# Key and query lengths through logarithms in the decay exponents, and a new order of units around the delta rule

## What is computed

```
qkv = silu(causal_depthwise_conv(proj[..., :1536], conv_qkv));  q, k, v = split(qkv)
q = q * rsqrt(sum(q^2) + 1e-6) * 128 ** -0.5        # per token and head
k = k * rsqrt(sum(k^2) + 1e-6)
g = -(exp(a_log) * softplus(a + dt_bias));  beta = sigmoid(bt);  g_cum = cumsum(g) in the chunk
decay = exp(where(causal, g_cum[i] - g_cum[j], -inf))
kk = strict_lower((beta k) k^T * decay)
u, k_cum = (I + kk)^-1 [v * beta, beta k * exp(g_cum)]
qk = (q k^T) * decay;  q_dec = q * exp(g_cum);  k_end = k * exp(g_cum[last] - g_cum)
for each chunk: v_new = u - k_cum S;  o = q_dec S + qk v_new
                S = S * exp(g_cum[last]) + k_end^T v_new
o = o * rsqrt(mean(o^2) + 1e-6) * gdn_norm;   y_a = o * silu(z)
```

## Time and profile before

| | |
|---|---|
| Median of 3 runs | 1255.66 us (1255.56 to 1256.26) |
| Profiled execution | 1255.7 us, span 1254.0 us |
| TensorE matmul busy | 1213.0 us (97% of the span) |
| VectorE, ScalarE, GpSimd busy | 390.5, 243.5, 148.7 us |
| DMA | 453.45 MB, mean 362 GB/s |
| Token mixer | to about 318 us |
| Experts | from about 340 us to 1246 us |

### The profile page before, as it was taken

One profiled execution on the slowest core, in us unless ns is written; L12 is line 12 of the kernel. 1 busy time (PEld: TensorE's weight loads), 2 busy tenths in 40 slices (PEclk: granted clock), 3 DMA queues, 4 the chain that ended last, 5 costly groups with the idle time before them and its releaser, 6 DMA issues.

```text
span 1254.0 us, 17233 instructions
## 1 busy us (share of the span) xinstructions
PE 1213.0 (97%) x7155; PEld 613.1 (49%) x7155; DVE 390.5 (31%) x768; ACT 243.5 (19%) x402; POOL 148.7 (12%) x106
## 2 busy tenths in 40 slices
PE   8999999999999999999999999999999999999995
PEld 8999999998733333333333333333333333333332
DVE  6675633335522222222222222222222222222224
ACT  5764354544210000000000000000010000000001
POOL 7454323555100000000000000000000000000000
PEclk9999999999999999999999999999999999999999
DMA  9644231875899999999999999999999999999994
GB/s 335 221 148 143 70 136 67 330 292 201 353 409 429 428 429 428 427 429 429 429 428 429 429 429 428 429 428 430 428 429 427 427 427 428 429 427 428 428 427 198
DMA packets 53388, 453.45 MB, mean 362 GB/s; under 512 B 6925, under 2 KB 7002, under 8 KB 28762
## 3 DMA queue, kind: packets, MB, share of 16 engines
q1 hardware_dynamic: 53338, 452.71, 87.0%
HBM read 451.64 MB, written 1.05 MB: 361 GB/s over the span
## 4 chain that ended last, share of the span: by engine, by line
PE 78%; DMA 8%; SPq 5%; DVE 3%; ACT 3%; issue 2%; POOL 0%; DVEq 0%; ACTq 0%
PE bank L1419 29%; PE bank L1491 15%; DMA late<-in_w_gate_up_dram 8%; PE bank L1209 6%; SPq L807 5%; PE bank L1210 5%; PE bank L1211 5%; PE bank L1504 4%; PE bank L1390 4%; PE bank L1405 2%; PE bank L1479 1%; ACT late L1181 1%; ACT w_hi L1069 1%; PE bank L1499 1%; DMA raw<-in_w_mem_kv_dram 0%
## 5 line engine op out<-in xcount | busy, mean ns | idle before, releaser
L1419 PE MATMUL bank<-late 128*64 128x512 f32 x1536 | 343.5, 595 | 5.4 <-DMA late<-in_w_gate_up_dram 5.4
L1491 PE MATMUL bank<-late 128*64 128x512 f32 x1024 | 229.6, 601 | 6.0 <-ACT late L1181 6.0
L1419 PEld LDWEIGHTS bank<-late 128*64 128x64 f32 x1536 | 106.7, 137 | 223.2 <-issue 209.6
L1491 PEld LDWEIGHTS bank<-late 128*64 128x64 f32 x1024 | 71.3, 138 | 142.4 <-issue 128.6
L1209 PE MATMUL bank<-act_hi,w_hi 128*128 128x256 f32 x448 | 129.5, 289 | 1.9 <-DVE early L1699 1.4
L1210 PE MATMUL bank<-act_lo,w_hi 128*128 128x256 f32 x448 | 125.8, 281 | 0.0
L1211 PE MATMUL bank<-act_hi,w_lo 128*128 128x256 f32 x448 | 125.7, 281 | 0.0
L1834 DVE TENSOR_SCALAR late<-bank 128x512 f32<-128x512 f32 x32 | 22.1, 692 | 308.9 <-PE bank L1419 308.9
L1419 PE MATMUL bank<-raw,late 128*64 128x512 f32 x512 | 116.7, 598 | 1.5 <-DMA raw<-in_w_gate_up_dram 1.5
L770 POOL TENSOR_TENSOR w_lo<-raw,w_hi 128x1024 fp32r<-128x1024 f32 x33 | 81.9, 2483 | 102.1 <-ACT w_hi L1069 102.0
L1209 PEld LDWEIGHTS bank<-act_hi,w_hi 128*128 128x128 f32 x448 | 84.3, 188 | 4.1 <-DVE early L1699 2.0
(11 more groups left out here) (321 smaller groups left out, 1186.4 us busy)
## 6 DMA issues: line engine op xcount, KB each, us to landing
late<-in_w_gate_up_dram SPq DMA_DIRECT2D x96, 2048.0 KB, 37.1
late<-in_w_down_dram SPq DMA_DIRECT2D x64, 2048.0 KB, 36.5
raw<-in_w_gate_up_dram SPq DMA_DIRECT2D x32, 2048.0 KB, 35.2
raw<-in_w_in_dram SPq DMA_DIRECT2D x8, 2048.0 KB, 9.0
early<-in_w_in_dram SPq DMA_DIRECT2D x6, 2048.0 KB, 8.1
raw<-in_w_br_dram SPq DMA_DIRECT2D x3, 2048.0 KB, 7.6
raw<-in_w_mem_kv_dram SPq DMA_DIRECT2D x8, 512.0 KB, 11.2
raw<-in_w_o_dram SPq DMA_DIRECT2D x1, 2048.0 KB, 8.5
```

Source lines behind the costliest of these rows:

```text
L1419: ins = mm(bk[64 * c:64 * c + 64, :], x_slotT[:, k % 4, 64 * (k // 4):64 * (k // 4) + 64], w[:, kk, at + 512 * c:at + 512 * (c + 1)], star ...
L1491: ins = mm(ps[3][64 * c:64 * c + 64, :], hidT[:, kk, 64 * q:64 * q + 64], w[:, kk, c * 512:(c + 1) * 512], start=(q == 0 and kk == 0), sto ...
```

## The change

The lengths of k and q are no longer multiplied into k and q. The sum of squares of k goes through a logarithm: half of it is added to g_cum (`log_k`), which enters the exponents of decay and of k_end; exp(-0.5 log) times beta (`beta_k`) takes beta's place where beta stood for k. The sum of squares of q acts only on the epsilon of the last norm (`o_eps`), since that norm takes any factor of a row out. The step lengths is gone, with its 16 matmuls and its VectorE and ScalarE work, and norms now writes one column for each (token tile, head) and not 128.

The squares are made by GpSimd, one head at a time, during qkv 1 to 8 (12 operations for 8 heads). The first half of the step order is new: norms stands right after qkv 11, then xc 0, logs, xc 1, the exponential and log decay, xc 2, scalars, xc 3, decay, gc 0, ScalarE's part of decay, gc 1, gc 2, **scores, gc 3, tokens, gb 0, lx0**, gb 1, lx1, gb 2, xlx1, gb 3, lx2, qm 0, xlx2, qm 1, lx3, qm 2, xlx3, qm 3, lx4, z 0, xlx4, z 1, lx5, z 2, xlx5, z 3, kcum. The z slots of weights move behind qm accordingly. Only ScalarE's parts of norms and decay stand one unit behind their products (steps `ga`).

```diff
-    ["scalars", "decay", "norms", "lengths", "scores", "tokens"]
+    ["norms", "scalars", "decay", "scores", "tokens"]
...
-    order += [("qkv", 0), ("qkv", 1), ("ab", 0), ("qkv", 2), ("abT", 0), ("qkv", 3), ("decay functions",)]
-    order += [("qkv", 4), ("qkv", 5), ("log decay",), ("qkv", 6), ("qkv", 7)] + [("g", "scalars"), ("qkv", 8), ("qkv", 9), ("g", "decay")]
-    order += [("qkv", 10), ("qkv", 11)]
...
-    long = [(kind, n) for kind in ("z", "xc", "gc", "gb", "qm") for n in range(4)]
+    order += [("qkv", 0), ("qkv", 1), ("ab", 0), ("qkv", 2), ("abT", 0)] + [("qkv", n) for n in range(3, 12)]
+    order += [("decay functions",), ("g", "norms")]
+    long = [(kind, n) for kind in ("xc", "gc", "gb", "qm", "z") for n in range(4)]
+    at = {("xc", 0): [("logs",)], ("xc", 1): [("ga", "norms"), ("log decay",)], ("xc", 2): [("g", "scalars")],
+          ("xc", 3): [("g", "decay")], ("gc", 0): [("ga", "decay")], ("gc", 1): []}
     for unit in long:
-        order += [unit]
-        if unit not in (("xc", 0), ("xc", 2)):
-            order += [("g", g.pop(0))]
+        order += [unit] + (at[unit] if unit in at else [("g", g.pop(0))])
         if unit[0] == "qm":
             order += [("score", unit[1])] + ([("soft", unit[1] - 1)] if unit[1] else [])
...
# ScalarE
+                act.wait_ge(g_act, GA["norms"] - 1)
+                a.activation(beta_k, log_k, ACT.Exp, scale=-0.5).then_inc(g_act, 1)
+            elif name == "logs":
+                a.activation(t_b, t_b, ACT.Ln, bias=1.0).then_inc(ab_act, 1)
                 act.wait_ge(g_pe, GP["norms"])
-                for t in range(NT):
-                    for n in range(2):
-                        ins = a.activation(inv_norm[:, t, 4 * n:4 * n + 4], ps[4 + 2 * t + n][:, 0::P], ACT.Sqrt,
+                a.activation(log_k, ps[5][:, 0:NPB].rearrange("p (t h) -> p t h", t=NT), ACT.Ln,
...
# TensorE
-                        ins = mm(out4(t * 2 * H + n), squares[:, n, t * P:(t + 1) * P], ones[:], start=True, stop=True)
-            elif name == "lengths":
-                pe.wait_ge(g_dve, GD["norms"])
-                for n in range(2 * H):
-                    for t in range(NT):
-                        ins = mm(ps[4 + n // 2][:, (n % 2) * T + t * P:(n % 2) * T + (t + 1) * P],
-                                 spread(inv_norm, t, n), ident[:], start=True, stop=True)
+                        ins = mm(ps[4 + n // H][:, at:at + 1], squares[:, n, t * P:(t + 1) * P], ones[:, 0:1], start=True, stop=True)
...
             elif name == "scores":
-                pe.wait_ge(g_dve, GD["lengths"])
+                pe.wait_ge(g_dve, GD["decay"])
+                pe.wait_ge(g_act, GA["decay"] - 2)
...
# VectorE, step scalars
+                v.wait_ge(g_act, GA["norms"])
+                step(d.tensor_tensor(beta_k, beta_k, beta, ALU.mult))
                 v.wait_ge(g_pe, GP[name])
                 step(d.tensor_copy(gcum, ps[3][:, 0:NPB].rearrange("p (t h) -> p t h", t=NT)))
+                step(d.scalar_tensor_tensor(out=log_k, in0=log_k, scalar=0.5, in1=gcum, op0=ALU.mult, op1=ALU.add))
...
# VectorE, step scores (the eight operations behind the wait are unchanged)
                 v.wait_ge(g_act, GA["decay"])
-                step(d.tensor_tensor(bexp, bexp, beta, ALU.mult))
+                step(d.tensor_tensor(bexp, bexp, beta_k, ALU.mult))
                 step(d.tensor_copy(chunk_decay, expg[:, :, CHUNK - 1::CHUNK]))
-                v.wait_ge(g_act, GA[name])
-                d.reciprocal(inv_norm, inv_norm).then_inc(g_dve, 1)
...
# VectorE, step olen
-                d.tensor_reduce(o_ss, LT, AX.X, ALU.add).then_inc(g_dve, 1)
+                step(d.tensor_reduce(o_ss, LT, AX.X, ALU.add))
+                d.scalar_tensor_tensor(out=o_ss, in0=o_ss, scalar=1.0 / DH, in1=o_eps.rearrange("p t h -> p (t h)"),
+                                       op0=ALU.mult, op1=ALU.add).then_inc(g_dve, 1)
...
# GpSimd
+                if s[0] == "qkv" and 1 <= s[1] <= 2 * H:
+                    c = s[1] - 1
+                    pool.wait_ge(silu_done, c + 1)
+                    if c < H:
+                        for k in range(2):
+                            src = halves(qkvT[:, c, :])[:, :, 1 - k, :]
+                            ins = eng.tensor_tensor(halves(squares[:, c, :])[:, :, k, :], src, src, ALU.mult)
+                    else:
+                        ins = eng.tensor_tensor(squares[:, c, :], qkvT[:, c, :], qkvT[:, c, :], ALU.mult)
+                    ins.then_inc(squared, 1)
...
# VectorE
-                    if c == 11:
-                        v.wait_ge(silu_done, 12)
-                        d.tensor_tensor(squares, qkvT[:, 0:2 * H, :], qkvT[:, 0:2 * H, :], ALU.mult).then_inc(g_dve_sq, 1)
```

More of the change, by code:

```diff
@@ L110, in mixer_schedule @@
     order += [("ab split",)]
[L111 to L116 removed]
+    order += [("qkv", 0), ("qkv", 1), ("ab", 0), ("qkv", 2), ("abT", 0)] + [("qkv", n) for n in range(3, 12)]
+    order += [("decay functions",), ("g", "norms")]
+    g = [s for s in GDN_STEPS if s not in ("norms", "scalars", "decay", "olen", "onorm")]
+    long = [(kind, n) for kind in ("xc", "gc", "gb", "qm", "z") for n in range(4)]
+    at = {("xc", 0): [("logs",)], ("xc", 1): [("ga", "norms"), ("log decay",)], ("xc", 2): [("g", "scalars")],
+          ("xc", 3): [("g", "decay")], ("gc", 0): [("ga", "decay")], ("gc", 1): []}
     for unit in long:
[L118 to L120 removed]
+        order += [unit] + (at[unit] if unit in at else [("g", g.pop(0))])
         if unit[0] == "qm":
             order += [("score", unit[1])] + ([("soft", unit[1] - 1)] if unit[1] else [])
[L123 removed]
+        if unit == ("z", 0):
+            order += [("soft", H - 1)]
     attention = [("pT", 0), ("pT", 1), ("ym", 0), ("pT", 2), ("ym", 1), ("pT", 3), ("ym", 2), ("ym", 3)]
@@ L127, in mixer_schedule @@
         order += [attention.pop(0)]
-        order += [("g", s) for s in g[:2 if len(g) > KD - n else 1]]
-        g = g[2 if len(g) > KD - n else 1:]
+        if len(g) >= KD - n:
+            order += [("g", g.pop(0))]
     assert not g and not attention
@@ L448, in hybrid_layer @@
             GP[name] = gp
-            ga += {"lx0": 0, "decay": 3, "norms": 1, "tokens": 1, "kcum": 1, "olen": 1}.get(name, 1 if name.startswith(("lx", "state")) else 0)
+            ga += {"lx0": 0, "decay": 3, "norms": 2, "tokens": 1, "kcum": 1, "olen": 1}.get(name, 1 if name.startswith(("lx", "state")) else 0)
             GA[name] = ga
-            gd += {"lx0": 1, "scalars": 1, "decay": 1, "norms": 1, "lengths": 1, "scores": 1, "tokens": 1, "olen": 2, "kcum": 1, "vnew0": 0, "state3": 0}.get(
+            gd += {"lx0": 1, "scalars": 1, "decay": 1, "norms": 1, "scores": 1, "tokens": 1, "olen": 2, "kcum": 1, "vnew0": 0, "state3": 0}.get(
                 name, 1 if name.startswith(("xlx", "vnew", "state")) else 0)
@@ L520, in chunk_T @@
                 return a[:, p % H, (p // H) * P:(p // H + 1) * P]
-            if name == "scalars":
+            if name == "norms":
+                pe.wait_ge(squared, 2 * H)
+                pe.wait_ge(h_split, 2 * NT)
+                for n in range(2 * H):
+                    for t in range(NT):
+                        at = t * H + n % H
+                        ins = mm(ps[4 + n // H][:, at:at + 1], squares[:, n, t * P:(t + 1) * P], ones[:, 0:1], start=True, stop=True)
+            elif name == "scalars":
                 pe.wait_ge(g_dve_scal, 1)
@@ L530, in pe_gdn @@
                 pe.wait_ge(g_dve, GD["scalars"])
-                pe.wait_ge(h_split, 2 * NT)
                 for p in range(NPB):
@@ L534, in pe_gdn @@
                 for p in range(NPB):
[L535 to L537 removed]
+                    ins = mm(out4(NPB + p), spread(beta_k, p // H, p % H), ident[:], start=True, stop=True)
+            elif name == "scores":
                 pe.wait_ge(g_dve, GD["decay"])
[L539 to L551 removed]
+                pe.wait_ge(g_act, GA["decay"] - 2)
                 for p in range(NPB):
@@ L647, in dve_gdn @@
                 ins.then_inc(g_dve, 1)
-            elif name == "norms":
+            elif name == "scores":
                 v.wait_ge(g_act, GA["decay"])
-                step(d.tensor_tensor(bexp, bexp, beta, ALU.mult))
+                step(d.tensor_tensor(bexp, bexp, beta_k, ALU.mult))
                 step(d.tensor_copy(chunk_decay, expg[:, :, CHUNK - 1::CHUNK]))
-                v.wait_ge(g_act, GA[name])
-                d.reciprocal(inv_norm, inv_norm).then_inc(g_dve, 1)
[L655 to L665, removed]
                 v.wait_ge(g_pe, GP[name])
@@ L1167, in _ @@
                                      bias=r_neg[:, t:t + 1], accum_out=r_sum[:, t:t + 1]).then_inc(r_exp, 1)
-                elif kind == "g":
+                elif kind == "logs":
+                    act_gdn(act, "logs")
+                elif kind == "ga" or kind == "g" and s[1] not in ("norms", "decay"):
                     act_gdn(act, s[1])
@@ L1665, in _ @@
                     continue
```

(2 more changed lines are left out.)

29 lines of the change are left out of this document (18 added, 11 removed).

## The result

The changed kernel takes 1259.81 us (median of 15 runs, 1256.96 to 1262.44), the kernel before 1255.56 us (15 runs, 1254.18 to 1258.20). The ratio is 1.0033 with a 95% interval of 1.0026 to 1.0040: slower by 0.33%, about 4 us. The profiled execution is one of the three fastest of its kernel: 1257.03 us, span 1255.3 us. It stands only 1.3 us above the profiled execution before. So the traces explain less than the medians differ by; what of the rest is known stands further down.

The account below looks back on a forecast made before the run. TensorE was taken to bound the mixer, whose length sets the start of the experts' weight stream and so the end. Removed 5.5, added waits 6.35 and clock 1.2 gave +2.1 us on 1255.7: 1257.8 us, range 1253.6 to 1260.3.

Parts of the forecast that it names:

- the rival of the squares: qkv 3 to 8: GpSimd's squares meet VectorE's low parts, 0.4 us a unit, 2.4 in all, 1260.2 us; chance 0.13.
- The bound: Experts' weight stream: what moves its start, 315.57 us before, moves the end one for one; TensorE sets the mixer's time.
- What goes: TensorE in the mixer: step lengths 3.58 us and idle times of 0.81, 0.25 and 0.82 removed, 5.5 in sum.
- 0.81: Idle TensorE at 81.55, where ScalarE's part of decay holds back the copies of qkv 10: claimed to go.
- 0.25: Idle TensorE at 62.26 us, ahead of scalars: claimed to go.
- 0.40 and 0.41: Waits ahead of lx3 and lx4, from a gb unit's convolution ahead of the xlx results: claimed to go, 0.82 us together.
- Tokens: TensorE ahead of tokens: 4.9 us idle, since one unit covers scores' VectorE work; bounds 2.7 and 6.
- Other waits: Added besides tokens: lx1 0.5 us, lx2 0.4, scalars and decay 0.3, the last norm 0.25.
- Scalars and decay: ScalarE's decay functions, logs and exponential after qkv 11: chain done 0.3 us after xc 3; bounds 0 and 1.28.
- The last norm: Step olen: one more small VectorE operation on a chain TensorE waits for, 0.25 us; bounds 0.1 and 0.42.
- The clock: Clock falls after the idle time ahead of tokens: 1.2 us counted, bounds 0 and 2.2; no-fall rival 1256.6, chance 0.20.
- (a): Lengths goes, 3.58 us; norms with single columns gains nothing, with 1 us allowed in the range.

Follow-up runs that it names:

- scores_early: The changed kernel with step scores moved from behind gc 2 to behind gc 1: 1252.47 us, ratio 0.9976 to the kernel before.
- lo_both: The changed kernel with the low part of piece 29 on GpSimd and of piece 30 on VectorE: 1256.25 us, ratio 1.0002 to the kernel before.
- lo30_dve: The changed kernel with the low part of piece 30 on VectorE instead of GpSimd: 1258.30 us, ratio 1.0015 to the kernel before.
- the pair of kernels: Changed kernel, scores behind gc 1, 64 columns in norms: with the 16 lengths products put back unread 1254.17 us, without them 1251.56 us.
- again: The changed kernel unaltered, run once more for a second profile: 1259.99 us, ratio 1.0030 to the kernel before.
- norms64: The changed kernel with 64 columns instead of one for each product of norms: 1258.91 us, ratio 1.0024 to the kernel before.
- fill_tokens: The changed kernel with 18 unread products of ident by ident in the wait ahead of tokens: 1256.75 us, ratio 1.0011 to the kernel before.
- early_n64: The changed kernel with scores behind gc 1 and 64 columns in norms: 1249.74 us, ratio 0.9951 to the kernel before; repeated, 1251.56 us.

## Why the prediction was right, and what was mis-sized

The measured 1259.81 us lies in the range of 1253.6 to 1260.3, 2 us above the predicted 1257.8. But "within 0.2%" was given the larger chance, and the change is slower, beyond it. The stream's start, at 318.23 and 319.86, is later than the 317 to 318 that was to show the forecast. By its time the result is nearest to the rival of the squares (1260.2), whose mechanism isn't in the trace.

- **The bound.** The end follows the start of the stream. Over all profiles the way from there to the end is 936.4 to 938.8 us, while the start lies between 310.3 and 320.9. The longer ways (before, scores_early, lo_both, and lo30_dve with 938.0) are those with half clock near 330 and 360, as in the earlier trace rows. The changed kernel's profile has none there, and its way is 1.4 us shorter; this fits a span that grew by 1.3 only while its start moved by 2.66. So the end follows the start to within 2.4 us, and not exactly one for one.
- **What goes.** Confirmed: lengths (3.68 by the pair of kernels, 3.58 predicted), 0.81, 0.25, 0.40 and 0.41.
- **Tokens.** Predicted 4.9, measured 4.75, with its three parts nearly as they were worked out (2.7, 1.1 and 1.1, against 2.7, 0.9 and 1.1).
- **Other waits.** lx1 0.48 and lx2 0.40, as predicted. Scalars and decay: nothing instead of 0.3. The last norm: 0.11 more instead of 0.25.
- **GpSimd's squares.** Nothing, as predicted: TensorE has no idle time of 0.25 or more between 51 and 112, and the rival of the squares falls.
- **Loads of tables.** None of them reached TensorE.
- **The clock.** This is the term that was mis-sized. The half clock at tokens came, and costs 1.6 (tokens takes 3.55 instead of 1.97) where 1.2 was counted, within its bounds; the 0.79 ahead of lx0 stayed and covered none of it. The half clock behind norms was not in the sum: 1.4 us in the first profile, and twice its length in the second, whose stream starts 1.6 later still. The step that failed is (a): I asked only whether single columns would make norms faster, and gave them no price.

The sum of the measured terms for the start of the stream: -5.44 for what went (3.57 + 0.81 + 0.25 + 0.40 + 0.41), +4.75 +0.48 +0.40 +0.11 +1.6 +1.4 = +3.3; the trace has +2.66. Of the 0.6 between, 0.15 are shorter waits ahead of the attention scores (0.46 and 0.57 before, 0.42 and 0.46 after) and 0.11 is norms itself. The rest was not pursued.

What the traces leave open is the distance to the medians. The profiled spans differ by 1.3 and 2.4 us (first profile and again, each against the kernel before), the medians by 4.2. Twelve of the 15 timed runs have a mean clock of 0.987 to 0.992, against 0.993 in the three fastest, the profiled one among them; the kernel before has 0.991 to 0.996. The doubled half clock behind norms explains a step to 0.992 only (again). The one profile with 0.987, lo30_dve at 1260.19 us, has it too, and three more periods, at 301, 335 and 365 us. And ten of the 12 runs of norms64 have 0.988 to 0.992 as well, though no profile with 64 columns shows half clock behind norms. This points to half clock in the timed runs at places that the changed kernel's two traces don't show. But a timed run has no trace, and where it lies, and why more often than in the kernel before, stays open.

Of the table loads: each change between Exp and Ln has its load of 1.28 us in the changed kernel too, unlike the rule of the Trainium skill (ScalarE: Activation LUTs, "Table sets: the hidden batching unit"), by which one load serves both. They cost TensorE nothing here. Of the clock: by the Trainium skill (TensorE: Matmul & The Clock Gate, "Loop structure matters more than you think") the long wait drops the clock; the trace and fill_tokens agree, with 3.55 against 1.97 us for tokens.

## What to carry to other kernels

In an order written by hand, a step's cover is the number of units between it and the next, and the work of the other engines must be laid out beside it with what their queues put ahead: here 5.5 us stood under 2.83, behind one low part and beside another. A change that removes 3.6 us from the bounding engine and shifts one step by one place can be a loss; the same change with that step one place earlier is 0.24% faster than before. And a cheaper instruction on TensorE is not cheaper if the clock falls behind it: here one column in place of 64 saved 0.06 us and cost 1.4 in the profile.

## What was not expected of the hardware

- Norms with one column, 32 instructions in 3.46 us with no idle time, met 3.4 or 6.8 us at 1.2 GHz in all seven profiles that have it, from 75.6 to 77.8 us on, so in its last part or up to 1.2 us behind it. With 64 columns it took 3.52 us, and none of four profiles has such a period.
- TensorE's waits of 4.75 us were followed by half clock in every profile that has one. One of 3.62 us was too; waits of 2.65 and 2.71 us ahead of tokens were not, and the wait of 2.1 us that ends between 292 and 302 was in six profiles of thirteen. The length of the wait alone doesn't part the two cases.
- In these profiles a period of half clock lasts about 3.4 us or twice that, and the same kernel has it in one execution and not in another (early_n64 and its repetition). A single profile can therefore stand 2 or 3 us from the median of its kernel.
- The last pair of scores, which reads two SBUF tensors on VectorE, waits for the end of GpSimd's low part when the two meet. Beside the same low part (108.50 to 110.84) it ended at 112.0 whether it began at 109.57 (2.43 us) or at 108.66 (3.33 us); with none beside it, it took 1.29.
